# Eight ring slots and loop bodies of two batches for the experts of a transformer pair

## What is computed

```python
gate = g_w * jax.nn.softmax(top_val, axis=-1)          # top group, then top 2 of its 8 experts
...
def run_block(args):
    xb, e = args
    h = jax.nn.silu(xb @ w_gate[e]) * (xb @ w_up[e])
    return h @ w_down[e]
```

## Time and profile before

| | us |
|---|---|
| median of 3 runs | 1643.46 |
| lowest and highest | 1640.52, 1644.93 |
| the profiled execution, as timed | 1640.27 |
| its span, first to last instruction | 1638.5 |
| TensorE busy in it | 1223.2 |
| mean granted TensorE clock | 0.912 of full |

### The profile page before, as it was taken

How to read it: one execution, slowest core, us unless ns; L and a number is a source line. 1 busy time by engine, 2 the same in 40 slices (tenths; PEclk the granted TensorE clock), 3 DMA queues, 4 the chain that set the end, 5 groups by cost and what they waited for, 6 DMA issues and landing times.

```text
span 1638.5 us, 22054 instructions
## 1 busy us (share of the span) xinstructions
PE 1223.2 (75%) x9589; PEld 760.3 (46%) x9589; DVE 319.7 (20%) x722; ACT 249.8 (15%) x579; POOL 49.3 (3%) x82
## 2 busy tenths in 40 slices
PE   7999855655565665565566566557998999999997
PEld 4565633433332332333233233233445585888843
DVE  1532321211211221121121122112023213100000
ACT  3321311110110111111111011111002112100000
POOL 4101000000000000000000000001000000000000
PEclk9999988988988898897898888799998799999999
DMA  9315499999999999999999999999642051544300
GB/s 352 137 52 169 158 427 429 428 429 428 428 429 428 428 428 428 428 429 428 429 428 428 428 428 429 428 429 395 230 152 82 4 174 53 161 150 149 137 36 26
DMA packets 83105, 493.15 MB, mean 301 GB/s; under 512 B 4768, under 2 KB 28528, under 8 KB 58496
## 3 DMA queue, kind: packets, MB, share of 16 engines
q1 hardware_dynamic: 81088, 486.69, 72.7%
q0 software_dynamic: 1600, 5.17, 1.0%
q10 hardware_dynamic: 384, 0.82, 0.1%
HBM read 491.61 MB, written 1.05 MB: 301 GB/s over the span
## 4 chain that ended last, share of the span: by engine, by line
PE 47%; DMA 46%; DVE 2%; issue 1%; ACT 1%; SPq 1%; POOL 1%; POOLq 0%; DVEq 0%; ACTq 0%
DMA ring<-in_w_up_dram 45%; PE bank L539 11%; PE bank L900 10%; PE bank L1050 9%; PE bank L1081 5%; PE bank L618 3%; PE bank L559 1%; PE bank L638 1%; PE bank L581 1%; DMA ring<-in_w_in_dram 1%; PE bank L527 1%; PE bank L601 1%; SPq L372 1%; PE bank L755 0%; PE bank L589 0%
## 5 line engine op out<-in xcount | busy, mean ns | idle before, releaser
L900 PE MATMUL bank<-ring,big 128*32 128x256 f32 x4096 | 304.1, 462 | 252.6 <-DMA ring<-in_w_up_dram 235.3
L900 PEld LDWEIGHTS bank<-ring,big 128*32 128x32 f32 x4096 | 173.9, 132 | 377.9 <-issue 340.7
L914 PE MATMUL bank<-ring,big 128*32 128x256 f32 x2048 | 123.8, 382 | 75.5 <-DVE big L1687 62.1
L539 PE MATMUL bank<-ring,xT 128*128 128x512 f32 x384 | 166.8, 594 | 0.6 <-ACT xT L1117 0.6
L1050 PE MATMUL bank<-xT,ring 128*128 128x256 f32 (+1 forms) x832 | 153.3, 347 | 0.8 <-issue 0.8
L1050 PEld LDWEIGHTS bank<-xT,ring 128*128 128x128 f32 x832 | 138.0, 191 | 16.5 <-issue 1.6
L914 PEld LDWEIGHTS bank<-ring,big 128*32 128x32 f32 x2048 | 63.4, 109 | 135.9 <-DVE big L1687 78.9
L1682 DVE TENSOR_TENSOR big<-big,bank 128x128 f32<-128x128 f32 x64 | 23.8, 371 | 524.1 <-ACT big L1264 524.1
L539 PEld LDWEIGHTS bank<-ring,xT 128*128 128x128 f32 x384 | 72.8, 191 | 89.2 <-issue 89.1
L1264 ACT ACTIVATE big<-bank 128x128 f32<-128x128 f32 x64 | 17.8, 278 | 511.5 <-PE bank L900 511.5
L1691 DVE COPY big<-bank 32x256 f32<-32x256 f32 x128 | 54.3, 424 | 134.7 <-PE bank L914 133.9
(11 more groups left out here) (262 smaller groups left out, 847.5 us busy)
## 6 DMA issues: line engine op xcount, KB each, us to landing
ring<-in_w_gate_dram SPq DMA_DIRECT2D x64, 2048.0 KB, 18.3
ring<-in_w_up_dram SPq DMA_DIRECT2D x64, 2048.0 KB, 22.8
ring<-in_w_down_dram SPq DMA_DIRECT2D x64, 2048.0 KB, 25.2
ring<-in_w_gate_up_dram SPq DMA_DIRECT2D x22, 1024.0 KB, 6.8
ring<-in_w_in_dram SPq DMA_DIRECT2D x14, 1024.0 KB, 15.2
ring<-in_w_down_dram SPq DMA_DIRECT2D x8, 1024.0 KB, 6.9
ring<-in_w_in_dram SPq DMA_DIRECT2D x3, 2048.0 KB, 23.3
ring<-in_w_ckv_dram SPq DMA_DIRECT2D x2, 2048.0 KB, 12.9
```

The source lines that it names most:

```text
L539: i = pe.matmul(bank[(2 * u + t) % 4][:, 0:n], lhsT[:, k, t * P:(t + 1) * P], w[:, k, :], start=(k == 0), stop=(k == KD - 1))
L900: i = pe.matmul(bank[q % 2][TOK * j:TOK * (j + 1), 0:SEQ], xg[:, k, TOK * q:TOK * (q + 1)], w[:, :, k, j * P:(j + 1) * P], start=(k == 0), ...
L914: i = pe.matmul(bank[6 + q % 2][TOK * m:TOK * (m + 1), 0:SEQ], hT[:, q % 2, TOK * k:TOK * (k + 1)], w[:, k, SEQ * m:SEQ * (m + 1)], start= ...
```

## The change

The ring becomes one tile of 7 slots and 7680 columns. xT and mix, 2048 columns each, are now slot 6, and aux begins where slot 7 does, so that slot 7 is its first 4096 columns. The experts use all eight slots, in the order MOE_SLOTS = 4, 7, 5, 0, 1, 2, 6, 3; the other weights go on using six. The loads to slot 7 wait for gla_o and mix_n, those to slot 6 for route_mm and n2_n. Ahead of the loops stand eight loads instead of six.

As 12 units don't divide by eight slots, a loop body now holds two batches (PAIR = 8 experts, 24 units) and runs 8 times, on all engines; inside, the batch is written out twice (`half`). The counts `moe_gu` and `moe_d` start from 4 instead of 1, so that waits for two batches back stay positive.

Gate and up no longer always lie side by side. `hidden_pair` takes a view from the lower to the higher of the two slots and steps over what lies between (`w[:, 0:hi-lo+1:hi-lo]`). Where up has the lower slot, its result stands in the first half of the bank, and ACT and DVE read the halves the other way round (`gate_first`). The unchanged remainder of the batch is only indented, and is left out here.

```diff
-MOE_UNITS = [(part, q) for q in range(BATCH) for part in ("gate", "up", "down")]
-assert len(MOE_UNITS) == 2 * RING
+PAIR = 2 * BATCH
+NPAIR = NE // PAIR
+MOE_UNITS = [(part, e) for e in range(PAIR) for part in ("gate", "up", "down")]
+MOE_SLOTS = (4, 7, 5, 0, 1, 2, 6, 3)
+MRING = len(MOE_SLOTS)
+assert len(MOE_UNITS) % MRING == 0
+def unit_slots(e):
+    return [MOE_SLOTS[MOE_UNITS.index((part, e)) % MRING] for part in ("gate", "up")]
+def gate_first(e):
+    return unit_slots(e)[0] < unit_slots(e)[1]
...
-        counted["moe_gu"], counted["moe_d"] = ("moe_gu", 1, 1), ("moe_d", 1, 1)
+        counted["moe_gu"], counted["moe_d"] = ("moe_gu", BATCH, 1), ("moe_d", BATCH, 1)
...
-        ring = sb("ring", RING * SLOT)
+        ring = sb("ring", 7 * SLOT + 7680)
         x = sb("x", TT * D).rearrange("p (t d) -> p t d", t=TT)
         xn = sb("xn", TT * D).rearrange("p (t d) -> p t d", t=TT)
-        xT_ = sb("xT", KD * SEQ)
+        xT_ = ring[:, 6 * SLOT:6 * SLOT + KD * SEQ]
         xT = xT_.rearrange("p (k s) -> p k s", k=KD)
-        mix_ = sb("mix", TT * D)
+        mix_ = ring[:, 6 * SLOT + KD * SEQ:7 * SLOT]
         mix = mix_.rearrange("p (t d) -> p t d", t=TT)
         big = sb("big", 6144)
-        aux = sb("aux", 7680)
+        aux = ring[:, 7 * SLOT:]
...
+        def moe_slot(u):
+            return ring[:, MOE_SLOTS[u % MRING] * SLOT:(MOE_SLOTS[u % MRING] + 1) * SLOT]
...
-                sp.dma_start(slot(PRE_UNITS + u), w).then_inc(S(f"moe_in{u % RING}"), 16)
+                sp.dma_start(moe_slot(u), w).then_inc(S(f"moe_in{u % MRING}"), 16)
             def moe_slot_free(u, done):
-                part, q = MOE_UNITS[u - RING]
-                n = done + q + 1 if u >= RING else done - BATCH + q + 1
+                part, e = MOE_UNITS[u - MRING]
+                n = done + e + 1 if u >= MRING else done - PAIR + e + 1
                 sp.wait_ge(*at("moe_d" if part == "down" else "moe_gu", n))
             def experts_of(b, u):
-                return bass.ds(b * BATCH + MOE_UNITS[u][1], 1)
-
-
-            for u in range(RING):
-                if PRE_UNITS + u - RING == SCRATCH:
+                return bass.ds(b * PAIR + MOE_UNITS[u][1], 1)
+            for u in range(MRING):
+                g = MOE_SLOTS[u]
+                if g == SCRATCH:
+                    sp.wait_ge(*at("gqa_pv", len(GQA_PAIRS) * TT))
+                if g in (SCRATCH, 7):
                     sp.wait_ge(*at("gla_o", TT))
-                    sp.wait_ge(*at("gqa_pv", len(GQA_PAIRS) * TT))
                     sp.wait_ge(*at("mix_n", TT))
+                elif g == 6:
+                    sp.wait_ge(*at("route_mm", TT))
+                    sp.wait_ge(*at("n2_n", TT))
                 else:
-                    sp.wait_ge(*at(*slot_read[PRE_UNITS + u - RING]))
+                    sp.wait_ge(*at(*slot_read[g + RING if g + RING in slot_read else g]))
                 moe_load(u, bass.ds(MOE_UNITS[u][1], 1))
-            with sp.Fori(0, NB - 1) as b:
-                for u in range(RING, 2 * RING):
-                    moe_slot_free(u, b * BATCH)
+            with sp.Fori(0, NPAIR - 1) as b:
+                for u in range(MRING, len(MOE_UNITS)):
+                    moe_slot_free(u, b * PAIR)
                     moe_load(u, experts_of(b, u))
-                for u in range(RING):
-                    moe_slot_free(u, b * BATCH + BATCH)
+                for u in range(MRING):
+                    moe_slot_free(u, b * PAIR + PAIR)
                     moe_load(u, experts_of(b + 1, u))
-            for u in range(RING, 2 * RING):
-                moe_slot_free(u, (NB - 1) * BATCH)
-                moe_load(u, experts_of(NB - 1, u))
+            for u in range(MRING, len(MOE_UNITS)):
+                moe_slot_free(u, (NPAIR - 1) * PAIR)
+                moe_load(u, experts_of(NPAIR - 1, u))
...
-                    part, q = MOE_UNITS[u + RING]
-                    sp.wait_ge(S("moe_d" if part == "down" else "moe_gu"), rounds * NE + (q + 2 - BATCH))
+                    part, e = MOE_UNITS[len(MOE_UNITS) - MRING + MOE_SLOTS.index((G2 + u) % RING)]
+                    sp.wait_ge(S("moe_d" if part == "down" else "moe_gu"), rounds * NE + (e + 1 + BATCH - PAIR))
...
+            with pe.Fori(0, rounds) as c, pe.Fori(0, NPAIR) as b:
+                pair = c * NPAIR + b
+                for half in range(2):
+                    it = pair * 2 + half
+                    def arrive(part, q):
+                        u = MOE_UNITS.index((part, half * BATCH + q))
+                        pe.wait_ge(*at(f"moe_in{u % MRING}", pair * (16 * len(MOE_UNITS) // MRING) + 16 * (u // MRING + 1)))
+                    def hidden_pair(q):
+                        arrive("gate", q)
+                        arrive("up", q)
+                        lo, hi = sorted(unit_slots(half * BATCH + q))
+                        w = ring[:, lo * SLOT:(hi + 1) * SLOT].rearrange("p (s k c) -> p s k c", s=hi + 1 - lo, k=KD)
+                        w = w[:, 0:hi + 1 - lo:hi - lo]
+                        for k in range(KD):
+                            for j in range(4):
+                                i = pe.matmul(bank[q % 2][TOK * j:TOK * (j + 1), 0:SEQ], xg[:, k, TOK * q:TOK * (q + 1)],
+                                              w[:, :, k, j * P:(j + 1) * P], start=(k == 0), stop=(k == KD - 1),
+                                              tile_position=(0, TOK * j))
+                        i.then_inc(S("moe_gu"), 1)
...
+                        A(eg[:, q % 2, :], bank[q % 2][:, 0:P] if gate_first(half * BATCH + q) else bank[q % 2][:, P:2 * P],
+                          ACT.Silu).then_inc(S("moe_e"), 1)
...
-            V.memset(stat[:, 122:123], 0.0).then_inc(S("moe_gu"), 1)
-            V.memset(stat[:, 123:124], 0.0).then_inc(S("moe_d"), 1)
+            V.memset(stat[:, 122:123], 0.0).then_inc(S("moe_gu"), BATCH)
+            V.memset(stat[:, 123:124], 0.0).then_inc(S("moe_d"), BATCH)
...
+                            up = bank[q % 2][:, P:2 * P] if gate_first(half * BATCH + q) else bank[q % 2][:, 0:P]
```

More of the change, by code:

```diff
@@ L406, in _ @@
             with sp.If(rounds > 1):
-                with sp.Fori(1, rounds) as c, sp.Fori(0, NB) as b:
-                    for u in range(2 * RING):
-                        moe_slot_free(u, c * NE + b * BATCH)
+                with sp.Fori(1, rounds) as c, sp.Fori(0, NPAIR) as b:
+                    for u in range(len(MOE_UNITS)):
+                        moe_slot_free(u, c * NE + b * PAIR)
                         moe_load(u, experts_of(b, u))
@@ L884, in _ @@
             rounds = pe.value_load(rounds_i[0:1, 0:1], min_val=1, max_val=MAX_ROUNDS)
[L885 to L897, removed]
-                    for k in range(KD):
[L899 to L946, removed]
-                                  ).then_inc(S("moe_cmb"), 1)
@@ new lines, in _, with down @@
+            with pe.Fori(0, rounds) as c, pe.Fori(0, NPAIR) as b:
[17 more added lines that the diff above has]
+                        i.then_inc(S("moe_gu"), 1)
+                    def down(q):
+                        arrive("down", q)
+                        w = moe_slot(MOE_UNITS.index(("down", half * BATCH + q))).rearrange("p (k c) -> p k c", k=4)
+                        pe.wait_ge(*at("moe_hT", it * BATCH + q + 1))
+                        if q >= 2:
+                            pe.wait_ge(*at("moe_y_a", it * BATCH + q - 1))
+                            pe.wait_ge(*at("moe_y_v", it * BATCH + q - 1))
+                        for k in range(4):
+                            for m in range(4):
+                                i = pe.matmul(bank[6 + q % 2][TOK * m:TOK * (m + 1), 0:SEQ],
+                                              hT[:, q % 2, TOK * k:TOK * (k + 1)], w[:, k, SEQ * m:SEQ * (m + 1)],
+                                              start=(k == 0), stop=(k == 3), tile_position=(0, TOK * m))
+                        i.then_inc(S("moe_d"), 1)
+                    pe.wait_ge(*at("moe_sel", it + 1))
+                    for t in range(TT):
+                        i = pe.transpose(bank[5][:, t * P:(t + 1) * P], sel_gate[:, t, :], ident)
+                    i.then_inc(S("moe_selT_tp"), 1)
+                    pe.wait_ge(*at("moe_xadd", it * 4 + 1))
+                    for k in range(KD):
+                        for t in range(TT):
+                            i = pe.matmul(bank[2 + k // 4][:, (k % 4) * P:(k % 4 + 1) * P], xn[:, t, k * P:(k + 1) * P],
+                                          sel[:, t, :], start=(t == 0), stop=(t == TT - 1))
+                        if k % 4 == 3:
+                            i.then_inc(S("moe_xg_mm"), 1)
+                    pe.wait_ge(*at("moe_xg_a", it + 1))
+                    pe.wait_ge(*at("moe_xg_v", it + 1))
+                    for q in range(BATCH):
+                        hidden_pair(q)
+                        down(q)
+                    pe.wait_ge(*at("moe_selT", it + 1))
```

(31 more changed lines are left out.)

97 lines of the change are left out of this document (40 added, 57 removed).

## The result

The changed kernel takes 1647.40 us (median of 20 runs, 1643.89 to 1650.62); the kernel before, beside it on the same chips, 1644.72 (20 runs). The ratio is 1.0018, 95% interval 1.0010 to 1.0025: about 2.7 us slower. The forecast was 4.4 us faster. One run of the kernel before, among the 21 beside e5 to e7, took 3158.53 us; it is in the slow state and is left out of their ratios.

A forecast was written before the change was run, and what follows sets the result against it. The prediction took the experts' weight-load stream as the bound: -9.8 us for two early loads, +5.4 for refetched code, sum -4.4, giving 1639.1 us against the median of 1643.46; range 1632 to 1645, chance 0.48.

The forecast's parts named there:

- What bounds the kernel: Expert stage: the stream of 192 weight loads, 4.89 us each at 428.6 GB/s, sets the end; TensorE follows it.
- Two more slots: Ahead of the expert loops: eight loads instead of six land early, taking 2 x 4.89 = 9.8 us off the stream's end.
- Rival C: Ahead of the loops: slots not both filled in time, only 4.9 us gained, time 1644.0; chance 0.06.
- Double load at 133.4: Loads 2 and 3 go out together beside the router's weights; cost nothing, with 20 us of cover.
- strided operand: Gate and up product reading slots further apart: at most half as much again of 3.7 us, taken as 0.
- half the back edges: Expert loops with bodies of two batches: the back edges' time lies beside the stream, so halving them changes nothing.
- Nine packets refetched per pass: TensorE's doubled loop body: each of seven returns fetches all nine code packets again, 63 in all, about 90 on q8.
- rival A: TensorE's loop: the code stays or its fetching is free, time 1633.7; chance 0.38.
- The price of a packet: Expert stream: each code packet fills one engine 1.10 us; 63 spread over sixteen engines plus one packet cost 5.4 us.
- Rival B: Expert stream: refetched packets hit the same few engines, at most 2.2 us seven times, +5.6 net, 1649; chance 0.08.
- Its own signs: Trace signs: last up load near 1107, beyond 1111.5 by B; prediction wrong if a mid-loop slice falls under 427 GB/s.
- The tail: From the last up load's landing at 1111.5 to the next block's first product at 1125.99; spans around the stage keep their length.

The follow-up runs named there:

- e5: Changed kernel plus 32 tiny 4 x 4 matmuls (128 instructions) on TensorE, placed where it waits anyway: 1634.27 us, ratio 0.9945 to the kernel before.
- e7: Changed kernel with loop bodies of four batches instead of two: 1645.23 us, ratio 1.0008 to the kernel before.
- e4: Changed kernel with 128 more TensorE wait instructions, and loads 7 and 8 held until the first expert's gate and up product: 1654.91 us, ratio 1.0063 to before.
- e1: Changed kernel with 128 more already met wait instructions on TensorE before its first input product: 1644.43 us, ratio 0.9999 to the kernel before.
- e6: Changed kernel with six slots instead of eight, plus 32 tiny matmuls (128 instructions) on TensorE: 1644.38 us, ratio 1.0019 to the kernel before.
- e8: Kernel before with eight loads ahead of the loop and the first batch written out; one-batch loop over six slots kept: 1631.77 us, ratio 0.9918.
- e10: The changed kernel unaltered, run again for a second trace: 1644.17 us in its one run.
- e2: Changed kernel with the six slots of the kernel before, doubled loop bodies kept: 1658.34 us, ratio 1.0086 to the kernel before.
- e3: Changed kernel with 64 more already met wait instructions on TensorE before its first input product: 1650.76 us, ratio 1.0039 to the kernel before.

## Why the prediction was wrong, point by point

**What bounds the kernel: right.** In every kernel here the end follows the last landing by 521.8 to 524.3 us, and where no packet of code falls into the stream a load takes 4.89 us in all of them.

**Two more slots, -9.8: right.** e4 against e1 10.5, e6 against e5 10.1, e8's last landing 9.76 earlier. Loads went out in the order and, but for the run's own start, at the times foretold. Rival C fell: in after the 9th load was the first behind the gap. One reading beside it was short: in before the load issued at 169.4 landed only at 177.8, so the queue was not yet empty at 177.3; with 12 us to the next issue nothing hung on it.

**Double load at 133.4, strided operand, half the back edges: nothing, right.** From the first expert load to the first refill pass 80.3 us in before, and 80.3 to 80.4 in e5, e7 and e10, which have the double load. e6 holds the doubled body alone and is within what can be measured of before. The far slots cost the product nothing: its mean in this stage is 459 ns, as against 462 over the nearer ones, at the same granted clock of 0.86 from 214 to 1118 us (busy 302.6 us over the same 4096).

```profile
L926 PE MATMUL bank<-ring,big 128*32 128x256 f32 x4096 | 302.6, 459 | 219.5 <-DMA ring<-in_w_up_dram 204.0
```

**Nine packets refetched per pass: right.** Foretold were 63 packets at the returns and about 90 on q8; the trace has 63 and 92. The step before it was not sound, though: a body of 6.7 packets that begins inside one lies in seven or in eight, and the prediction took eight as given. That it was eight is luck of where the body starts; 128 instructions on (e1, e5) it would have been seven, and rival A's time of 1634 with it. Packets of after between one return and the next, from the times of q8's packets and TensorE's branches:

```
until 296.7: 13;  then 9, 9, 9, 9, 9, 9, 9;  after the loop (1132.4): 16
```

The Trainium skill, "Runtime: NRT & Kernel Launch", section "Instruction fetch mechanics", gives TensorE 128 KiB, refilled as a FIFO in blocks of 16 KiB, which makes eight blocks. The runs agree, and more sharply than the prediction could say: a body over eight blocks and the one fetched ahead is fetched whole each time (after, e2, e3), over seven and one never (e1, e5, e6). The same section of the Trainium skill calls the crossing of a 16 KiB boundary mostly hidden. For TensorE running straight on that held: the only idle time on "issue" that after has and e5 hasn't is the 5.5 us at each return. For the stream of the other transfers it did not hold.

**The price of a packet: the step that failed.** The prediction took the 1.10 us that a packet fills on one engine, spread the 63 evenly over sixteen engines (4.3), added one packet, and got 5.4. Measured are 12. Both factors of the term were off, the delay of the engine that carries a packet (that it strikes) and the number of engines struck:

- A packet puts the engine it strikes back by some 1.54 us, not 1.10. Each slip is one such step: 1.53, 1.53, 1.55, 1.53, 1.48, 1.66, 1.49, 1.53 in e10, and 1.52 to 1.55 in after.
- The packets strike eight of the sixteen engines, not all, and in turn: their durations in after repeat with a period of eight, 1018, 1073, 1078, 1060, 1099, 1099, 1095, 1016 ns and then the same again within some ns, although nine come in a pass. Sixteen engines' landings of one load late in the stage, in us behind the last of them:

```
before, load at 1111.5:  -1.8 -1.7 -1.7 -1.7 -1.7 -1.6 -1.5 -1.0 -0.9 -0.7 -0.7 -0.5 -0.1 -0.1 -0.0 0
e10,    load at 1115.6: -11.7 -11.6 -11.5 -11.5 -11.3 -11.1 -11.0 -11.0 -3.2 -3.0 -3.0 -2.6 -1.5 -1.4 -0.9 0
```

Eight engines have run ahead by what the stream lost, the other eight stay together. A load is there when its last engine is. So the stream slips by 1.54 us once in eight packets, 0.19 us a packet: 67 packets in the stream make 12.9, of which 12 are seen since the last round isn't full (8 rounds, 12.3). In time it fits too: nine packets in a pass of 119.4 us are eight in 106, and after's slips lie 106 us apart on average (320.0, 429.2, 543.3, ... 1064.9).

With this the sum is -9.8 + 12.1 = +2.3, and the medians gave +2.7. The argument for even spread, "packets would be expected to be spread like everything else", was an assumption and no row. Rival B had the better mechanism (some engines struck again and again, each load waiting for the slowest), and its point of decision, 1.4 us a pass, was passed: 12.1 / 7 = 1.7. It was given 0.08 because it was thought of as the worst end and not as what a rotation over few engines does. The three packets in the trace of before would have told the size of a strike: each moved one engine's landing by about 1.45 us, and three never struck the same one, so that the engines' own spread of 1.8 us took them up. I read their duration and not their effect.

**Its own signs.** Two of the signs named ahead came: slices of the stream under 427 GB/s (down to 417), which was to show the prediction wrong, and a last up load beyond 1111.5 (1118.7), which was B's. The first was set too sharply for the forecast itself, whose 63 packets and 5.4 us would also have taken the slices to some 426.

**The tail: right within a run's scatter.** From the last up landing to the second block's first product 14.5 and 15.5 us in the traces of before, 15.7 and 14.3 in those of after.

**What stays open.** Why a packet of 1.10 us costs its engine 1.54 (a longer load packet beside it, or a turn lost in the queue, weren't told apart). In e2 the eight engines don't show: all sixteen land within 3.1 us, and its slips come in part as pairs of 0.6 and 0.9; the sum per packet is the same, and its packets' durations have the period of eight too. Its queue holds fewer loads, so that no engine may be able to run far ahead, but that was not tried. In e3 the lead of the eight ends at 8 us though 12 are lost, and in e7 the slips come as pairs of 0.8 and 0.5. And the start of e8.

## What to carry to other kernels

Before a loop body is made longer, count the blocks of code that it touches (its instructions by where it starts, not by its size alone). On TensorE seven stayed here and eight did not: 128 instructions of shift were worth 13 us. The count on q8 tells which case it is. Where the DMA queues are the bound, as here, price a packet of code by how far it puts back the engine it strikes and by how few engines take turns, not by its bytes over all of them. And a gain at the start of a loop needs no change in the loop: with the first batch written out ahead of it (e8), the two early loads brought their 9.8 us and nothing was refetched.

## What the runs showed of the hardware

- Packets of TensorE's code come to eight of the sixteen DMA engines in turn, each setting its engine back by 1.5 us beside a full stream; eight unstruck engines ran 10 to 13 us ahead by the end in after, e10 and e7, 8 in e3.
- A body of TensorE that touches seven blocks of 256 instructions was returned to seven times without a packet (e5, q8 29); one that touches eight was fetched whole each time, nine packets (after, q8 92).
- Met semaphore waits are not free where TensorE is on the path: 64 instructions of them (e3) delayed the experts' first load by 2.5 us against after and 4.0 against e10, 128 (e1) by 8.25 and 9.8. As tiny products, partly under waits, 128 instructions left the first refill at 203.5, inside the range of the kernels without them (202.3 to 206.0).
- The stall at the return to a body that isn't held is 5.5 us each (38.6 over 7), hidden here by the wait for the loads.
